# A fused two-block transformer stack: the first in-projection started chunk by chunk behind the first norm

## The reference

```python
mod_lat = [m[:, None, :] for m in jnp.split(jax.nn.silu(c) @ ada_w[i] + ada_b[i], N_MOD, axis=-1)]
a_lat = modulate(rmsnorm(h_lat, g_pre), mod_lat[0], mod_lat[1])     # h * (1 + scale) + shift
b_gate, c_gate, v = jnp.split(a_lat @ w_in, 3, axis=-1)             # 1024 x 3072
y = (b_gate * depthwise_conv3(c_gate * v, conv_w)) @ w_out
h_lat = h_lat + mod_lat[2] * rmsnorm(y, g_post)
...
f = squared_relu_mlp(modulate(rmsnorm(h_lat, ...), mod_lat[3], mod_lat[4]), mlp_w_in, mlp_w_out)
```

## Time and profile before

| | |
|---|---|
| median of three runs | 1806.07 us (1805.27 to 1807.39) |
| profiled execution | 1808.28 us |
| its span | 1806.5 us |
| TensorE busy | 1732.5 us, 96% of the span |
| VectorE busy | 1076.4 us, 60% |
| ScalarE busy | 692.6 us, 38% |
| mean granted TensorE clock | 0.974 of full |

### The profile page before, as it was taken

The page is one execution under the profiler, slowest core; times in us unless marked ns, Lnnn a source line. Parts: engine busy times, 40 slices in busy tenths (PEclk is TensorE's granted clock), DMA queues, the critical chain, the costliest instruction groups (busy, mean ns, idle before and its releaser), DMA issues.

```text
span 1806.5 us, 21398 instructions
## 1 busy us (share of the span) xinstructions
PE 1732.5 (96%) x7642; PEld 1396.3 (77%) x7642; DVE 1076.4 (60%) x1648; ACT 692.6 (38%) x1000; POOL 132.7 (7%) x131
## 2 busy tenths in 40 slices
PE   4899999999999988999999999999998999999998
PEld 4788877888888766877888888877665788888887
DVE  5698756343434445465664564568998566366364
ACT  2222225232323241483442342336666444144242
POOL 0000000000000004000000000002894000000000
PEclk7699989999999998999999999999999999999999
DMA  7467512322222303201223232232220223322222
GB/s 241 152 222 232 163 47 72 112 96 93 93 93 93 111 24 94 71 25 47 93 93 117 86 100 93 87 91 78 70 70 24 72 92 105 104 93 93 93 82 82
DMA packets 182192, 176.18 MB, mean 98 GB/s; under 512 B 3160, under 2 KB 181596, under 8 KB 182124
## 3 DMA queue, kind: packets, MB, share of 16 engines
q1 hardware_dynamic: 182124, 175.29, 30.4%
HBM read 173.15 MB, written 2.10 MB: 97 GB/s over the span
## 4 chain that ended last, share of the span: by engine, by line
PE 90%; DVE 4%; issue 2%; ACT 2%; DMA 1%; DVEq 0%; SPq 0%; ACTq 0%
PE PSUM L1305 24%; PE PSUM L1306 23%; PE PSUM L1307 23%; PE PSUM L1612 2%; PE PSUM L1631 1%; PE PSUM L1633 1%; PE PSUM L1632 1%; PE PSUM L1350 1%; PE PSUM L1335 1%; PE PSUM L1495 1%; PE PSUM L1477 1%; PE PSUM L1520 1%; PE PSUM L1522 1%; PE PSUM L1521 1%; DMA XROW<-in_x 1%
## 5 line engine op out<-in xcount | busy, mean ns | idle before, releaser
L475 ACT ACTIVATE WH<-RAW 128x1024 fp32r<-128x1024 f32 x280 | 287.2, 1052 | 759.9 <-PE PSUM L1307 751.9
L1305 PE MATMUL PSUM<-XH,WH 128*128 128x512 f32 x1232 | 483.4, 392 | 11.9 <-issue 10.8
L1306 PE MATMUL PSUM<-XL,WH 128*128 128x512 f32 x1232 | 480.6, 390 | 0.0
L1307 PE MATMUL PSUM<-XH,WL 128*128 128x512 f32 x1232 | 480.5, 390 | 0.0
L828 DVE TENSOR_TENSOR WL<-RAW,WH 128x1024 fp32r<-128x1024 f32 x280 | 343.6, 1251 | 10.0 <-ACT WH L475 10.0
L1305 PEld LDWEIGHTS PSUM<-XH,WH 128*128 128x128 f32 x1232 | 232.0, 188 | 64.4 <-issue 15.7
L1305 PE MATMUL PSUM<-HH,WH 128*128 128x512 f32 x692 | 270.3, 391 | 6.7 <-DVE HL L1186 4.9
L1306 PEld LDWEIGHTS PSUM<-XL,WH 128*128 128x128 f32 x1232 | 232.1, 188 | 48.8 <-issue 1.2
L1307 PE MATMUL PSUM<-HH,WL 128*128 128x512 f32 x692 | 269.5, 389 | 0.0
L1306 PE MATMUL PSUM<-HL,WH 128*128 128x512 f32 x692 | 269.5, 389 | 0.0
L1307 PEld LDWEIGHTS PSUM<-XH,WL 128*128 128x128 f32 x1232 | 231.9, 188 | 48.4
(11 more groups left out here) (250 smaller groups left out, 1763.6 us busy)
## 6 DMA issues: line engine op xcount, KB each, us to landing
RAW<-in_ffn_w_up SPq DMA_DIRECT2D x44, 1024.0 KB, 5.0
ARAW<-in_ada_w SPq DMA_DIRECT2D x24, 1024.0 KB, 5.3
RAW<-in_mlp_w_in SPq DMA_DIRECT2D x16, 1024.0 KB, 5.4
RAW<-in_mlp_w_out SPq DMA_DIRECT2D x16, 1024.0 KB, 5.1
RAW<-in_ffn_w_down SPq DMA_DIRECT2D x16, 1024.0 KB, 4.9
RAW<-in_sc_w_in SPq DMA_DIRECT2D x12, 1024.0 KB, 5.2
RAW<-in_even_w_in SPq DMA_DIRECT2D x8, 1024.0 KB, 5.7
RAW<-in_odd_w_pw SPq DMA_DIRECT2D x16, 512.0 KB, 4.7
```

Of the source, the lines that this page charges most:

```text
L475: act.activation(WH[:, j, a:b, :], RAW[:, j, a:b, :], ACT.Copy).then_inc(s_hi, 1)
L1305: pe.matmul(o, wh, mh[:, k, :], start=(k == 0), stop=False)
L1306: pe.matmul(o, wh, ml[:, k, :], start=False, stop=False)
L1307: mm = pe.matmul(o, wl, mh[:, k, :], start=False, stop=(k == kn - 1))
```

## The change

Shift unit i and scale unit 4+i belong to chunks 2i and 2i+1 of x. The change works in four steps i. Each makes the scale and shift of its two chunks, splits them, and multiplies the three first in-projection units by them, in turn, with the shift products of the next step between. Unit 2 has buffers of its own (`RAW_3`, `WH_3`, `WL_3`) and banks 6 and 7. The three units' weights come in pieces of two chunks (256 KB). All scale units are summed by DVE, all shift units by TensorE. `ARAW_2`, a second pair of modulation buffers, lies where `XROW` is, so its first load waits until x is turned. Squares of x are now summed by TensorE instead of DVE (`square_to_sum`), two shift products behind each. x is loaded before the first modulation unit, the other vectors behind the pieces of step 2, and they are turned after unit 0's end. Eighteen matmuls of the identity stand before the turning of x; the two `keep_busy` matmuls go. Modulation units 8 to 23 are spread over windows 2 to 14 instead of 0 to 11. Separately, `first_two` lets the first two down-projection units of a last group run their chunks 0 to 3 before either runs its others.

```diff
+FIRST = 3
+WINDOW_MODS = {2: (8,), 3: (9, 10), 4: (11,), 5: (12,), 6: (13, 14), 7: (15,), 8: (16,), 9: (17, 18), 10: (19,),
+               11: (20,), 12: (21,), 13: (22,), 14: (23,)}
+
+
+def halves(u, n):
+
+    return u * 2 + (n - 2 * FIRST)
+
+
+def pieces(i, u):
+
+    return FIRST * i + u + 1
...
+            def load_first_mod(i, part):
+
+
+                a = (4 + i, i)[part]
+                if i == 1:
+                    sp.wait_ge(s_xt, DC)
+                elif i >= 2:
+                    sp.wait_ge((s_ad, s_ap)[part], i - 1)
+                dst, done = ((ARAW, s_ar), (ARAW_2, s_ar2))[i % 2]
+                sp.dma_start(dst[:, part], ada[:, :, a * UW:a * UW + UW]).then_inc(done[part], 16)
+
+            def load_first_pieces(i):
+
+                for u in range(FIRST):
+                    sp.dma_start(first_unit(u, i)[0], scin[:, 2 * i:2 * i + 2, order[u]:order[u] + UW]
+                                 ).then_inc(s_raw0[i], 16)
...
-            load_mod(0)
-            load_mod(1)
             sp.dma_start(XROW[:, :, :], x_rows).then_inc(s_xin, 16)
+            load_first_mod(0, 0)
+            load_first_mod(0, 1)
+            load_first_pieces(0)
+            load_first_mod(1, 0)
+            load_first_mod(1, 1)
+            load_first_pieces(1)
+            load_first_mod(2, 0)
+            load_first_mod(2, 1)
+            load_first_pieces(2)
...
+            load_first_mod(3, 0)
+            load_first_mod(3, 1)
+            load_first_pieces(3)
+            for u in range(FIRST, 16):
                 if u < 12:
                     load(u, u % 2, scin, order[u % 3] + u // 3 * UW)
                 else:
                     load(u, u % 2, scout, (u - 12) * UW)
-                if u < 4:
-                    load_mod(6 + u)
-                else:
-                    for a in window_mods(u - 4):
-                        if a + 2 < 24:
-                            load_mod(a + 2)
+                if u == FIRST + 1:
+                    load_mod(8)
+                    load_mod(9)
+                for a in WINDOW_MODS.get(u - 4, ()):
+                    load_mod(a + 2)
+            load_mod(23)
...
+            first_hi(0)
             act.wait_ge(s_const, 1)
             rms(ST_X0, 1.0 / D)
-            for u in range(2):
-                hi_half(u, u, 0)
-                hi_half(u, u, 1)
-            act.wait_ge(s_sm, 3)
-            split_shift(0, S_GS0, S_MOD)
+            for i in range(4):
+                act.wait_ge(s_sm, 3 * i + 4)
+                split_shift(0, S_GS0, S_MOD, (2 * i, 2 * i + 1))
+                if i < 3:
+                    first_hi(i + 1)
```

DVE (`scaled_x` is L863's operation, `first_lo` three pieces of WL, `turned_vectors` a copy of turned vectors):

```diff
+            turned_vectors(0)
+            dve.wait_ge(s_const, 7)
+            dve.wait_ge(s_ve, 1)
+            dve.tensor_scalar(sc_(S_B1, 8), col("ada_b", 8, 8), 1.0, None, ALU.add).then_inc(s_sm, 1)
+            dve.wait_ge(s_cs, 1)
+            mod_unit(4)
+            for c in range(DC):
+                dve.wait_ge(s_xt, c + 1)
+                dve.tensor_copy(X[:, c, :], PS_[:, c % 4, :]).then_inc(s_xu, 1)
+            first_lo(0)
+            dve.wait_ge(s_r, ST_X0 + 1)
+            scaled_x(0)
+            scaled_x(1)
+            for i in range(4):
+                dve.wait_ge(s_ap, i + 1)
+                dve.wait_ge(s_ac, i + 1)
+                for n in (2 * i, 2 * i + 1):
+                    dve.tensor_scalar(sc_(S_GS0 + n), PS_[:, COL_BANK, 8 + n:9 + n], sc_(S_B1 + n), col("gains", n),
+                                      ALU.add, ALU.mult).then_inc(s_sm, 1)
+                tt(sc_(S_MOD + 2 * i, 2), PS_[:, COL_BANK, 2 * i:2 * i + 2], col("ada_b", 2 * i, 2), ALU.add).then_inc(s_sm, 1)
+                for c in (2 * i, 2 * i + 1):
+                    dve.wait_ge(sp_h, c + 1)
+                    tt(XL[:, c, :], TF[:, c % 2, :], XH[:, c, :].bitcast(F32), ALU.subtract).then_inc(s_x, 1)
+                if i < 3:
+                    scaled_x(2 * i + 2)
+                    scaled_x(2 * i + 3)
+                    mod_unit(5 + i)
+                    first_lo(i + 1)
...
-                lo_half(u + 2, j, 0)
-                lo_half(u + 2, j, 1)
+                if u:
+                    lo_half(u + 2, j, 0)
+                    lo_half(u + 2, j, 1)
                 if u % 3 == 2:
                     for c in range(2):
                         n = 2 * step + c
                         dve.wait_ge(c_h, n + 1)
                         tt(HL[:, n, :], TA[:, c, :], HH[:, n, :].bitcast(F32), ALU.subtract).then_inc(s_h, 1)
-                for a in window_mods(u):
+                for a in WINDOW_MODS.get(u, ()):
                     mod_unit(a)
```

TensorE:

```diff
+            def shift_products(i, first, last):
+
+
+                src, landed = ((ARAW, s_ar), (ARAW_2, s_ar2))[i % 2]
+                if first == 0:
+                    pe.wait_ge(landed[1], 16 * (i // 2 + 1))
+                    pe.wait_ge(s_cs, 1)
+                for step in range(first, last):
+                    n, k = step // 8, step % 8
+                    mm = pe.matmul(PS_[:, COL_BANK, 2 * i + n:2 * i + n + 1], src[:, 1, k, n * P:n * P + P],
+                                   sc_(S_CS + k), start=(k == 0), stop=(k == 7))
+                if last == 16:
+                    mm.then_inc(s_ap, 1)
...
+                raw, hi, lo = first_unit(u, k // 2)
+                mm = None
+                for c in range(2):
+                    wh, wl = (w[:, k % 2, c * P:c * P + P] for w in (hi, lo))
+                    o = PS_[:, (0, 2, 6)[u] + c, :]
+                    pe.matmul(o, wh, XH[:, k, :], start=(k == 0), stop=False)
+                    pe.matmul(o, wh, XL[:, k, :], start=False, stop=False)
+                    mm = pe.matmul(o, wl, XH[:, k, :], start=False, stop=(k == 7))
+                return mm
...
+            turn_vectors(0)
+            for _ in range(18):
+                pe.matmul(PS_[:, 7, 0:P], IDENT[:, :].bitcast(F32), IDENT[:, :].bitcast(F32), start=True, stop=True)
+            pe.wait_ge(s_xin, 16)
+            for c in range(DC):
+                if c >= 4:
+                    pe.wait_ge(s_xu, c - 3)
+                for b in range(TB):
+                    tr = pe.transpose(PS_[:, c % 4, b * P:b * P + P], XROW[:, b, c * P:c * P + P],
+                                      IDENT[:, :].bitcast(F32))
+                tr.then_inc(s_xt, 1)
+            pe.wait_ge(s_ve, 1)
+            for m in range(DC):
+                square_to_sum(ST_X0, m)
+                shift_products(0, 2 * m, 2 * m + 2)
+            scale_columns(0)
+            for i in range(4):
+                pe.wait_ge(s_x, 2 * i + 1)
+                if i < 3:
+                    for u in range(FIRST):
+                        pe.wait_ge(s_lo0, pieces(i, u))
+                        first_product(u, 2 * i)
+                        shift_products(i + 1, (0, 6, 11)[u], (6, 11, 16)[u])
+                    scale_columns(i + 1)
+                    pe.wait_ge(s_x, 2 * i + 2)
+                    for u in range(FIRST):
+                        first_product(u, 2 * i + 1)
+                else:
+                    for u in range(FIRST):
+                        pe.wait_ge(s_lo0, pieces(i, u))
+                        first_product(u, 6)
+                        pe.wait_ge(s_x, 8)
+                        first_product(u, 7).then_inc(s_mm, 1)
+                        if u == 0:
+                            pe.wait_ge(s_vin, 16 * (7 + 4 + 2 + 8))
+                            pe.wait_ge(s_sm, 13)
+                            pe.wait_ge(s_r, ST_X0 + 1)
+                            for t in range(1, VT):
+                                turn_vectors(t)
+            for u in range(FIRST, 12):
                 product(u, u % 2, XH, XL, 8, s_x, 0)
...
+            def first_two(u, base_, kn):
+
+
+                for k0, k1, j in ((0, 4, 0), (0, 4, 1), (4, kn, 0), (4, kn, 1)):
+                    if k0 == 0:
+                        pe.wait_ge(s_ev, u + j - 1)
+                    pe.wait_ge(s_lo, halves(u + j, k0 // 4 + 1))
+                    for k in range(k0, k1):
+                        pe.wait_ge(s_h, base_ + k + 1)
+                        for c in range(2):
+                            wh, wl = (w[:, j, k, c * P:c * P + P] for w in (WH, WL))
+                            o = PS_[:, 2 * j + c, :]
+                            pe.matmul(o, wh, HH[:, k, :], start=(k == 0), stop=False)
+                            pe.matmul(o, wh, HL[:, k, :], start=False, stop=False)
+                            mm = pe.matmul(o, wl, HH[:, k, :], start=False, stop=(k == kn - 1))
+                    if k1 == kn:
+                        mm.then_inc(s_mm, 1)
...
-                    if layer == 0 or first + steps < 11:
+                    if first + steps < 11:
                         h_units(u, 4, h + 2 * first, kn)
+                    elif layer == 0:
+                        first_two(u, h + 2 * first, kn)
+                        product(u + 2, 0, HH, HL, kn, s_h, h + 2 * first)
```

(6 more changed lines are left out.)

206 lines of the change are left out of this document (93 added, 113 removed).

## The result

| | before | changed |
|---|---|---|
| median of the runs (least to most), us | 1806.73 (1805.27 to 1807.69), 4 runs | 1790.57 (1789.03 to 1795.09), 4 runs |
| profiled execution: time, span, mean granted clock | 1808.28, 1806.5, 0.974 | 1789.03, 1787.2, 0.983 |

The ratio is 0.9914 (95% interval 0.9903 to 0.9926): the changed kernel is faster by 0.86%. The predicted median was 1793.4 with a range of 1786 to 1804.

A forecast was written before the change was run, and what follows sets the result against it. TensorE, with 90% of the chain, was taken as the bound; 8.5 us at the start plus 4.2 at the feed-forward ends, 12.7 off 1808.28, gave 1795.6, and 2.2 less for the median: 1793.4 us, range 1786 to 1804.

The forecast's parts named there:

- x ahead brings nothing by itself: At the start: VectorE sums unit 4 before copying x, so copies start at 17.2 us, against 17.12 before.
- Squares: Sum of squares before the in-projection: 1.43 us per square with two shift products, eight 11.5; first product at 38.4 us.
- Steps: Three full in-projection steps: 13.0 us each, 39.0 in all, with TensorE's work above VectorE's 11.8 and the loads' 8.
- Clock in step 0: First in-projection step starts at the low clock after TensorE idles from 33.2 to 38.4 us: costs 4.5 (2 to 9.3).
- Clock after the stall: Behind TensorE's 3.0 us stall before unit 3: low clock costs another 1.5 us (0 to 3).
- The new wait before unit 3: In-projection: VectorE's ZP, taps and WL take 5.7 us, unit 2 covers 2.7, so TensorE stands for 3.0.
- The down-projection: Feed-forward ends: waits of 2.9 and 2.0 us covered, less 0.7 for a late third unit: 4.2 us gained.
- Squares at the low clock: Rival at the start: squares take 21.2 us instead of about 12, +9, giving 1802 us; chance 0.12.
- One-column products take the clock down in every step: Rival in the in-projection steps: +8.7 us for each of three, less 4.5 counted, +21.6, giving 1815; chance 0.13.
- Loads or VectorE set the step: Rival in the in-projection steps: they set the pace, by 1 to 3 us each, giving 1799; chance 0.08.
- Gain given back in later windows: Rival: products start early, but windows 2 to 11, with VectorE time near 10.9 us, lose it: 1806; chance 0.04.
- Clock recovers at once: Rival: full clock returns immediately in step 0 and holds over the stall, -4 to -6 us, giving 1788; chance 0.10.

The follow-up runs named there:

- x third: Changed kernel with x loaded behind both first modulation loads, its place before the change: median 1795.52 us (1782.30 to 1796.47), ratio 0.9942 to the kernel before.
- scale before x: Changed kernel with scale unit 4 loaded before x, x second: median 1785.09 us (1779.36 to 1791.98), ratio 0.9879 to the kernel before.
- WL ahead: Changed kernel with the first half of unit 3's WL made before the taps on VectorE: median 1786.34 us, ratio 0.9887 to the kernel before.
- copies: Changed kernel with VectorE's eight copies of x before the sum of unit 4: median 1782.48 us, ratio 0.9854 to the kernel before.

## Why the prediction was right, and where it was off

- **Where the gain comes from: right.** It is the start (13.8 us by the marks) and the two ends of the feed-forwards (3.0 and 2.5), and nothing else.
- **x ahead brings nothing by itself: right in the work.** Landing 10.5 and 13.2 against 10.2 and 13.28, copies at 17.2 against 17.20. With the clock held up, the medians of the two orders differ by 0.2 us. What I missed is that the clock can fall and recover at other moments on the same work: with x third, single executions lie 14 us apart, and the median is 6 above that of x first.
- **Squares: mis-sized, by a row that mixes both clocks.** I took a shift product at 0.267 us for the high clock, from 16 products in 4.27 us. But the clock fell at 25.1, inside that row. Here are the kernel before in that stretch (TensorE alone) and five shift products of the changed kernel at 1.00:

```profile
22.27:25.00 2.73, 2.73 (x28) 1.00 1.10 354
25.20:26.54 1.34, 1.34 (x7) 0.50 0.89 284
...
57.29 1.17 PE L1436 MATMUL PSUM<-small,ARAW 128*128 128x1 f32 x10
```

  The last 1.4 us of the 4.27 ran at the low clock; at the high one a product takes 1.17 / 5 = 0.23. A square with two of them takes 1.30, not 1.43; the 0.06 beyond that is overlap with the next square. R stood at 32.97, not 34.2, and the first product at 37.03, not 38.4: 1.4 us.
- **Steps: mis-sized.** 13.0 predicted, 12.28 measured, for the same reason: eighteen one-column products at 0.04 us too much are 0.7. Three steps: 2.2 us. TensorE set the pace, no load or VectorE: from 36 to 92 us it waited only before the first product and before unit 3, so pieces of 256 KB cost nothing. The Trainium skill ("DMA: Bandwidth & Descriptors", anatomy of one DMA) states the fixed 2 us for loads that GpSimd issues; these are issued by SP. My 13.5 us had it on the three pieces only; paid in series by all five loads of a step it would make 18 (an estimate: 5 x 2 + 8). The steps took 12.28 without a wait for a load, so no such cost was paid in series.
- **Clock in step 0: right as a mechanism.** 4.5 predicted; 16.2 - 12.3 = 3.9 in the profiled execution. TensorE's busy time at the low clock is half lost, and by that the profiles give 1.5 us (x third: 2.9 us low) to 10.7 (scale before x: 21.4). My ends were 2 and 9.3.
- **Clock after the stall: possible, as I had it, but over-sized.** 1.5 (0 to 3) predicted, none in the changed kernel's profile. In four of nine profiles with the stall it fell and cost 1.7 to 3.1 us, 0.9 on the average.
- **The new wait before unit 3: right,** 3.0 predicted and 3.01 measured; moving WL gave back 3.1.
- **The down-projection: 4.2 predicted, 4.9 of waits gone by the trace,** 4.7 to 7.0 by ratios and medians. The deduction of 0.7 has no wait in the trace.

Put together, 1.4 + 2.2 + 0.6 + 1.5 make unit 3 earlier by 14.2 instead of 8.5 (measured 14.1 by the same mark), and with 0.7 more at the feed-forwards the gain is 19 instead of 12.7 for the profiled execution. The medians differ by 16.2 only: the profiled execution of before lay 1.6 over its median, that of the changed kernel 1.5 under. All five errors have the same sign. For the profiled execution the forecast was 1795.6, 6.6 us too high; that the median came within 2.8 us is luck in part, by which execution was profiled.

**The rivals.** Squares at the low clock: no, 1.00 from 22 to 34 us. One-column products take the clock down in every step: no, it held 1.00 from 46 to 88 us, and with the five matmuls through step 0 as well. The rule of the Trainium skill that I weighed there ("TensorE: Matmul & The Clock Gate", HAM oscillation) is about groups of matmuls with waits between them. I had applied it to the cut over K alone, which gave 1815. The trace doesn't bear that out: groups cut over K, with one-column products between them but no waits, ran at 1.00. A cut over K with waits between the groups is in no run here. Loads or VectorE set the step: no wait of that kind. Gain given back in later windows: no, the lead is 13.8 at the end of every unit from unit 3 to the end of the in-projection. Clock recovers at once: no in the changed kernel's profile (8 us into step 0), though nearly so in the one with x third.

## What to carry to other kernels

When a change moves work to a place where TensorE idled before it, count the clock as a term of its own with both ends, and then fill that idle stretch with throw-away matmuls: here 5 matmuls in 4.7 us of idling were worth 5 us by the medians (3.9 of it seen in step 0), and another place of one load moved the median by 6 us only as long as the stretch was empty. Before a row is used as the price of an instruction, look at the granted clock inside it: one row here was a third at the low clock, and that made each step 0.7 us too dear. And a clock that holds in one profile may fall at the same place in another. Compare such variants with the clock held, or the clock's moment will be read as the edit's worth. When three units end close together, look at what stands ahead of the next unit's preparation on VectorE: a stall of 3.0 us went by moving one instruction.

## What the runs showed of the hardware

- How long the clock stays low after an idle stretch differs between executions on the same work. From its fall before step 0, the profiles show it low for 6.8 us (x third), 10.2 (changed kernel, its repeat, and two more), 13.7 (WL ahead, without the feed-forward part, copies) and 24 (scale before x), with TensorE busy from the first product on in each. One edit that acts only a thousand microseconds later (without the feed-forward part) is among the 13.7, so there it isn't the edit that sets it. Later stretches vary in the same way: the one that begins at 226 to 250 us lasts 17.1 us in seven of the fourteen profiles (both kernels and twelve runs) and 13.7 in the others. Executions of the changed kernel lie near 1789 (clock 0.983) and near 1795 (0.980), with one at 1791.78 (0.982) between them; with x third they are at 0.988 and 0.979, 13 us apart or more. What decides it is not shown.
- An idle stretch of 3.0 us took the clock down in four of nine profiles, for 3.4 or 6.8 us; in three of them it fell only after TensorE had resumed, 0.5 to 0.7 us into unit 3. One of 4.7 us did in every profile of a changed kernel without the five matmuls, falling 0.8 to 4.0 us after the last matmul.
- What matmuls in a wait give depends on what comes behind it: 5 before the first product gave 5.4 us, 18 in the loads' wait nothing (what they sped up lay under a wait), 3 in the stall nothing that five executions can show.
- The clock column of the start can't be read before its first change. It says 1.00 for the first sixteen turnings of x both with the eighteen matmuls before them (1.97 us) and without (3.67 us).
